# GpSimd takes two of the eight last multiplies of a hybrid decoder layer, the pass flag is computed ahead of the gather, and the last group of each slice begins with its down step

## The reference

```python
x = x + concat(mlstm(h), sliding_window_attention(h)) @ w_out      # h = rmsnorm(x) @ w_in
x = x + hier_moe(rmsnorm(x, g_ffn), ...)     # top-1 of 4 groups, then top-2 of its 8 experts (32 in all)
gate = sigmoid(rmsnorm(x, g_ple) @ w_ple_gate)
x = x + gate * (p @ w_ple_proj)
y = rmsnorm(x, g_final)
```

## Time and profile before

| | us |
|---|---|
| median of three runs | 1517.54 |
| lowest and highest run | 1515.83, 1518.03 |
| the profiled execution's own time | 1517.73 |
| its span | 1516.0 |
| TensorE busy (matmul) | 1364.2 |
| VectorE busy | 350.8 |
| ScalarE busy | 252.4 |
| GpSimd busy | 31.4 |

### The profile page before, as it was taken

One profiled execution on the slowest core, in us unless ns is written; L12 is line 12 of the kernel. 1 busy time (PEld: TensorE's weight loads), 2 busy tenths in 40 slices (PEclk: granted clock), 3 DMA queues, 4 the chain that ended last, 5 costly groups with the idle time before them and its releaser, 6 DMA issues.

```text
span 1516.0 us, 22808 instructions
## 1 busy us (share of the span) xinstructions
PE 1364.2 (90%) x9764; PEld 859.7 (57%) x9765; DVE 350.8 (23%) x938; ACT 252.4 (17%) x558; POOL 31.4 (2%) x69
## 2 busy tenths in 40 slices
PE   9989999999999999987978787888788888999986
PEld 7878888888888543433523333333333356666655
DVE  3312221036621411301301010101010112222217
ACT  3201121041401322111101111110111111101015
POOL 1000000020022000000000000000000000000000
PEclk9999999999999999989989899899998999999998
DMA  9556333377978699999999999999999999999981
GB/s 343 204 169 227 118 132 113 138 279 264 375 291 371 268 427 401 426 427 428 426 427 428 428 429 429 428 429 428 428 429 428 429 413 427 426 426 428 427 345 58
DMA packets 64640, 527.50 MB, mean 348 GB/s; under 512 B 6030, under 2 KB 27926, under 8 KB 29350
## 3 DMA queue, kind: packets, MB, share of 16 engines
q1 hardware_dynamic: 63182, 525.27, 84.5%
q10 hardware_dynamic: 1384, 1.16, 0.2%
HBM read 512.33 MB, written 14.07 MB: 347 GB/s over the span
## 4 chain that ended last, share of the span: by engine, by line
DMA 42%; PE 26%; DVE 1%; issue 1%; ACT 1%; DVEq 0%; ACTq 0%
DMA raw<-in_w_up 26%; DMA more<-in_w_up 8%; PE ps L1944 7%; DMA raw<-in_w_down_cuts 7%; PE ps L2208 4%; PE ps L2182 4%; PE ps L154 4%; DMA more<-in_w_down_cuts 1%; PE ps L2192 1%; PE ps L1184 1%; PE ps L1968 1%; PE ps L1919 1%; PE ps L1957 1%; PE ps L1260 1%; PE ps L1239 0%
## 5 line engine op out<-in xcount | busy, mean ns | idle before, releaser
L154 PE MATMUL ps<-mixT_hT,raw 128*128 128x264 f32 x1920 | 436.1, 387 | 2.3 <-PEq L808 1.7
L154 PEld LDWEIGHTS ps<-mixT_hT,raw 128*128 128x128 f32 x1920 | 361.9, 190 | 67.1 <-issue 6.9
L1944 PE MATMUL ps<-raw,mixT_hT 128*32 128x512 f32 x1488 | 200.2, 669 | 90.7 <-DMA raw<-in_w_up 62.0
L1944 PEld LDWEIGHTS ps<-raw,mixT_hT 128*32 128x32 f32 x1488 | 43.0, 116 | 212.6 <-DMA raw<-in_w_up 88.3
L2208 PE MATMUL ps<-mixT_hT,more 128*128 128x264 f32 x512 | 126.1, 395 | 1.2 <-ACT mixT_hT L2289 1.2
L1199 DVE TENSOR_TENSOR mixT_hT<-ps,ffn_gain 128x512 f32<-128x512 f32 x33 | 22.8, 691 | 417.9 <-PE ps L1919 417.9
L2208 PEld LDWEIGHTS ps<-mixT_hT,more 128*128 128x128 f32 x512 | 94.9, 191 | 30.8 <-issue 16.4
L1184 PE MATMUL ps<-x_res,mine 128*32 128x512 f32 (+1 forms) x792 | 109.0, 668 | 0.0
L1957 PEld LDWEIGHTS ps<-fold,mixT_hT 128*128 128x128 f32 x512 | 69.3, 210 | 53.6 <-issue 35.2
L1919 PEld LDWEIGHTS ps<-ident,xe 128*64 128x64 f32 x1056 | 66.5, 217 | 28.3 <-issue 28.3
L1957 PE MATMUL ps<-fold,mixT_hT 128*128 128x32 f32 x512 | 76.6, 296 | 5.7 <-ACT mixT_hT L1766 5.7
(11 more groups left out here) (373 smaller groups left out, 905.5 us busy)
## 6 DMA issues: line engine op xcount, KB each, us to landing
raw<-in_w_gate SPq DMA_DIRECT2D x62, 2048.0 KB, 16.5
raw<-in_w_down_cuts SPq DMA_DIRECT2D x35, 2048.0 KB, 17.5
more<-in_w_up SPq DMA_DIRECT2D x32, 2048.0 KB, 15.4
raw<-in_w_up SPq DMA_DIRECT2D x31, 2048.0 KB, 16.9
raw<-in_mix_chunks SPq DMA_DIRECT2D x60, 1024.0 KB, 5.4
more<-in_w_down SPq DMA_DIRECT2D x16, 2048.0 KB, 22.4
more<-in_w_down_cuts SPq DMA_DIRECT2D x13, 2048.0 KB, 25.6
more<-in_w_gate_cuts SPq DMA_DIRECT2D x8, 2048.0 KB, 21.6
```

Source lines behind the costliest of these rows:

```text
L154: return nc.tensor.matmul(ps[:, j, 0:NT], core.raw[:, q % NCH, k * GW + j * P:k * GW + (j + 1) * P], xT[:, core.groups[g].k0 + c * CK + k, ...
L1944: last = nc.tensor.matmul(ps[own, (GATE, UP)[m], :], xT[:, k, i * SLOTS:(i + 1) * SLOTS], weights, start=(i == 0 and k < 4), stop=(i == EI ...
```

## The change

Three edits.

Routing: `before` is computed ahead of the wait for the ranks. The count goes into a bank of its own and stands ahead of the gather; the flag is computed right behind `mine`. Both `state(3, ...)` follow the gather.

```diff
-        state(3, 0)
-        gather_slots(core, pe, rt, shared, 0)
-        state(3, 1)
-        pe.wait_ge(q["r_before"], 1)
-        nc.tensor.matmul(ps[:, 0, 2 * P:2 * P + NE], core.ones[:], before[:, 2, :], ...)   # r_counted
+        pe.wait_ge(q["r_before"], 1)
+        nc.tensor.matmul(ps[:, 6, 0:NE], core.ones[:], before[:, 2, :], ...)               # r_counted
+        gather_slots(core, pe, rt, shared, 0)
+        state(3, 0)
+        state(3, 1)
```

The last group of each slice from 1 on:

```diff
-                elif j == GROUPS - 1:
-                    gates(c - 1, j)
-                    if c == LAST:
-                        most_total()
-                    down(c, j)
-                    sums(c, j)
                 else:
                     down(c, j)
                     gates(c - 1, j)
                     sums(c, j)
+        most_total()
```

```diff
-    STORES = ((0, 3), (3, 5), (5, 7), (7, 8))
+    STORES = ((2, 5), (5, 7), (7, 8))
+    OWN = 2
...
         for first, end in STORES:
-            sp.wait_ge(q["t_done"], end)
+            sp.wait_ge(q["t_done"], end - OWN)
+            store(first, end)
+            if end == PAIRS - 1:
+                sp.wait_ge(q["t_own"], OWN)
+                store(0, OWN)
...
-        for i in range(PAIRS):
+        for i in range(OWN, PAIRS):
...
+    def pool(gps):
+        gps.wait_ge(q["t_ready"], 2)
+        gps.wait_ge(q["y_weighted"], 2 * OWN)
+        for i in range(OWN):
+            own = slice(2 * i, 2 * i + 2)
+            nc.gpsimd.tensor_tensor(x[:, own, :], pre[:, own, :], wide(root), ALU.mult).then_inc(q["t_own"], 1)
```

More of the change, by code:

```diff
@@ L1513, in tensor @@
         pe.wait_ge(q["r_taken1"], 4)
+        pe.wait_ge(q["r_before"], 1)
+        nc.tensor.matmul(ps[:, 6, 0:NE], core.ones[:], before[:, 2, :], start=True, stop=True).then_inc(q["r_counted"], 1)
+        gather_slots(core, pe, rt, shared, 0)
         state(3, 0)
-        gather_slots(core, pe, rt, shared, 0)
         state(3, 1)
-        pe.wait_ge(q["r_before"], 1)
-        nc.tensor.matmul(ps[:, 0, 2 * P:2 * P + NE], core.ones[:], before[:, 2, :], start=True, stop=True).then_inc(q["r_counted"], 1)
     def scalar(act):
@@ L1614, in vector @@
         link(V.tensor_tensor(c[:, 9, :], rt["pick_r"][:, 0:3, 0], rt["pick_r"][:, 3:6, 0], ALU.add))
+        link(V.tensor_tensor(before[:, 1, :], both[:, 0, :], both[:, 1, :], ALU.add))
+        link(V.scalar_tensor_tensor(before[:, 2, :], both[:, 2, :], valid[:], before[:, 1, :], ALU.mult, ALU.add))
+        dve.sem_inc(q["r_before"], 1)
         dve.wait_ge(q["r_ranked"], 1)
@@ L1620, in vector @@
         dve.sem_inc(shared["pick_step"], 1)
+        dve.wait_ge(q["r_counted"], 1)
+        link(V.tensor_reduce(c[:, 8, 0:1], ps[:, 6, 0:NE], AX, ALU.max))
+        V.tensor_tensor(rt["flag"][:], c[0:1, 8, 0:1].to_broadcast([1, PASSES]), rt["level"][0:1, :], ALU.is_gt
+                        ).then_inc(shared["flag_ready"], 1)
         ranks = ps[:, 0, P:P + 3 * NE].rearrange("p (o e) -> p o e", o=1).to_broadcast([P, 2, 3 * NE])
         link(V.tensor_tensor(taken.rearrange("p (i t) e -> p i (t e)", i=2), ranks, pick[:].rearrange("p i t e -> p i (t e)"), ALU.mult))
-        link(V.tensor_tensor(before[:, 1, :], both[:, 0, :], both[:, 1, :], ALU.add))
-        link(V.scalar_tensor_tensor(before[:, 2, :], both[:, 2, :], valid[:], before[:, 1, :], ALU.mult, ALU.add))
-        dve.sem_inc(q["r_before"], 1)
         link(V.tensor_reduce(rt["rank"][:], taken, AX, ALU.add))
@@ L1629, in vector @@
         V.tensor_tensor(c[:, 5, :], c[:, 4, :], c[:, 3, :], ALU.subtract).then_inc(q["r_in2"], 1)
[L1630 to L1633, removed]
         dve.wait_ge(shared["gain_landed"], 16)
@@ L2063, in _ @@
             routing["pool"](pool)
+            finish["pool"](pool)
             pool.wait_ge(*routing["state_stored"])
@@ L2105, in finish_stage @@
     names = ("down_done y_taken sums_done block_ready x_added x_scaled squared totalled gate_done gate_taken "
-             "logit_ready gate_ready x_updated y_squared y_weighted t_scaled t_total t_root t_ready t_done t_stored").split()
+             "logit_ready gate_ready x_updated y_squared y_weighted t_scaled t_total t_root t_ready t_done t_own t_stored").split()
     q = {n: core.sem(n) for n in names}
@@ L2164, in sync, with store @@
         piece(LAST)
+        def store(first, end):
+            sp.dma_start(out_y[:, 2 * first:2 * end, :], x[:, 2 * first:2 * end, :]).then_inc(q["t_stored"], 16)
         for first, end in STORES:
-            sp.wait_ge(q["t_done"], end)
-            sp.dma_start(out_y[:, 2 * first:2 * end, :], x[:, 2 * first:2 * end, :]).then_inc(q["t_stored"], 16)
-        sp.wait_ge(q["t_stored"], 16 * len(STORES))
+            sp.wait_ge(q["t_done"], end - OWN)
[3 more added lines that the diff above has]
+                store(0, OWN)
+        sp.wait_ge(q["t_stored"], 16 * (len(STORES) + 1))
     def tensor(pe):
@@ L2409, in vector @@
             V.tensor_tensor(x[:, own, :], pre[:, own, :], wide(root), ALU.mult).then_inc(q["t_done"], 1)
-    return {"sync": sync, "tensor": tensor, "scalar": scalar, "vector": vector}
+    def pool(gps):
[4 more added lines that the diff above has]
+            nc.gpsimd.tensor_tensor(x[:, own, :], pre[:, own, :], wide(root), ALU.mult).then_inc(q["t_own"], 1)
+    return {"pool": pool, "sync": sync, "tensor": tensor, "scalar": scalar, "vector": vector}
 def projection_groups():
```

## The result

The changed kernel took 1518.65 us (median of 22 runs), the kernel before 1516.99 beside it. The ratio is 1.0013, with a 95% interval of 1.0007 to 1.0019: 2.0 us slower (1.1 to 2.9), where 0.75 faster was forecast. One run of the kernel before, at 1743.5, is a stray, left out of the ratio.

The account below looks back on a forecast made before the run. The prediction took the weight stream, moved by TensorE's start on expert 0, as the bound. Turn -0.75, clock -2.0, last group -0.5 and last multiplies +2.5 gave -0.75: 1516.8 us, range 1513.9 to 1519.9.

Parts of the forecast that it names:

- The bound: Weight stream: TensorE's start on expert 0 moves it one to one, for up to 2.6 us.
- Part 1: Routing, flag ahead of the gather: expert 0's turn starts 0.75 us earlier if the register load is hidden.
- Part 1b: Expert 0's first 48 matmuls: without idle time before the turn TensorE's clock stays up, saving 2.0 us.
- Part 2: Last group of slice 7, down first: sums start earlier and run without a start-up gap, saving 0.5 us.
- The cap: End of slice 7: the gate matrix's last piece lands at 1474.0, limiting the down-first gain to 0.7 us.
- Part 3: Last multiplies: GpSimd's two get in ahead of VectorE's third and delay the first store; +2.5 us.
- my list of signs: Expected observations; at the end, the first store 4.4 us after the reciprocal instead of 2.0.
- Sum: Whole kernel: -0.75 - 2.0 - 0.5 + 2.5 = -0.75 us, giving 1516.8; chance 0.42.
- the first rival: Clock still falls at expert 0's turn and GpSimd shuts VectorE out: +1.25, 1518.8 us; chance 0.22.

Follow-up runs that it names:

- delayed front: The kernel before with eight extra 128x512 matmuls ahead of the count, making expert 0's turn late; ratio 1.0032, +4.9 us.
- the change once more: The changed kernel itself, unedited, measured and profiled a second time against the kernel before; ratio 1.0004, +0.6 us.
- the earlier first store: The kernel before with five stores instead of four, the first of pair 0 alone; ratio 0.9994.
- all three together: The kernel before with flag ahead of the gather, last state behind expert 0's turn, down first in the last group, eight single stores; 0.9993, -1.1 us.
- Kept warm: The kernel before with two extra 128x512 matmuls behind the count, where TensorE waits for the flag; ratio 0.9995.
- down first alone: The kernel before with only the down step put first in the last group of each slice; ratio 0.9989, -1.7 us.
- the end alone: The kernel before with GpSimd multiplying pairs 0 and 1, VectorE pairs 2 to 7, and stores reordered; ratio 1.0016, +2.4 us.

## Why the prediction was wrong, step by step

- **The bound (the stream, moved by TensorE's start on expert 0, one to one): right for a delay, too simple for a gain.** The delayed front moved the time by 4.9 us for 4.84. An early start gets through to the last expert and is partly lost there. I named the pauses at 526 and 572 as the last before 1469 and read the slice at 413 GB/s as nothing; it runs from 1213 to 1251, and 37.9 x (1 - 413/428) is 1.3 us.
- **Part 1, -0.75 for the turn: right.** -0.80 in two profiles of the changed kernel, with the register load hidden.
- **Part 1b, -2.0 for the clock, passed on whole: the step that failed.** It rested on two stretches of one execution, one with a fall and one without. Over the profiles with the old front the clock fell in 6 of 7 (the delayed one apart, where it stayed up behind the same 1.4 us of idle time); with the early flag alone in front it stayed up in 4 of 5, and it fell in the one profile that was compared, where the term gave 0.3. The times say the same: the front and the last group together, which is the change without GpSimd's part, gave 0.5 us (1.8 at most), where my sum had 3.25.
- **Where the term exists, the end gets part of it.** In nine profiles expert 1 starts at 30.3 us from the ranks or less, 2.6 us earlier on average than in the six with the old front and a fall. Their landing is 1.0 us earlier on average, and between 2.6 us earlier and 0.1 later. The pause between 1205 and 1225 was 3.1, 2.2, 0.9, 0.8, 2.9, 2.7, 0.4, 1.9 and 2.3 us in them; behind 30.8 or more it was 0.4 to 0.6 in all seven. (The delayed one is left out of this: all of it is 4.8 us late, so its pause lies partly behind 1225.) The six pauses of 1.9 us or more are those in which the last expert's third product takes 2.6 to 3.4 us instead of 1.9, as in the change once more. In the other three it takes 1.9. Slow down steps alone don't do it: the earlier first store had 6.54 us for the two and a pause of 0.6. And the pause isn't all: all three together had one of 0.4 and passed on 1.15 of 3.0 us.
- **Part 2, -0.5: right.** From landing to product 5.13 to 5.20 us in eight profiles, 5.56 to 5.60 in seven with the old order; 0.44 was measured. The cap was real too: where GpSimd only wrote, the gate's piece landed at 1472.03, 6.1 us behind the step instead of 4.9, and the product followed at 1472.09, which takes the whole gain. Kept warm, with the old order, shows the same (5.83).
- **Part 3, +2.5: right** in mechanism, place and order; 2.2 was measured. (My sum moved the first store by 2.6 us, my list of signs by 2.4, from 2.0 to 4.4; it was 2.24.) GpSimd holds VectorE for 1.1 us each, not 1.3; that is what 528 elements take at the 2.1 ns of the estimate, without the rest of an instruction.
- **Sum.** -0.8 - 0.3 - 0.4 + 2.2 = +0.7 for the compared execution, with -0.5 + 0.5 of other differences; +0.6 was measured between the spans. Without the clock's 2.0 my own terms gave +1.25, and 1518.8 was the first rival, on the slower side; 1518.65 was measured. That it fits so closely is partly luck: the kernel before stood at 1516.99 beside it and not at 1517.54, so the measured difference is +2.0 (1.1 to 2.9), and the second measurement gave +0.6. I had it at 0.22 and the forecast at 0.42, because I took a state of the clock that differs from run to run for a property of the code.

Open: why an early start and a fall of the clock in the last expert go together (six of nine, and the delayed front, against none of seven). The clock changes at other moments in each execution, so an execution spared at the turn may be one that is hit later; no run here forces that, and it is not shown. Open too is the 1.7 us of down first alone, of which profiles show 0.4.

## What to carry to other kernels

Before an elementwise instruction with two SBUF operands goes to GpSimd beside VectorE, look whether VectorE's own have two as well: here each then waited for the other in turn, and what counted was the instruction that the first store waits for. At an end that streams its output at full rate, what counts is when the first store goes out and that the next ones follow before the engines run dry. More engines behind it bought nothing here (9.08 us against 9.06); smaller stores took 0.6 and 0.9 us off the end in the profiles, and only together with down first was the gain clear in the times. A gain from TensorE's clock that one profile shows belongs into the range, not into the sum, until several executions show it. And a gain early in a stream is only as good as every later pause: list them all, the small ones too.

## What was not expected of the hardware

- A waiting GpSimd gets its turn even against VectorE instructions queued without a gap: one each, in strict turn, in three profiles (VectorE 1.80 and 1.83 us in the one shown).
- The clock stayed at 1.00 behind 1.44 us without a matmul in the delayed front and behind 1.43 us in the end alone. It fell behind the same gap in the six other profiles with the end alone's front.
- Stores of 270 KB each ran at 386 GB/s where larger ones ran at 411; 0.3 us over 2.16 MB.
